# Smaller transfers and pieces at both ends, spare transposes in TensorE's waits, and other banks and operand offsets, in a kernel of two fp32 blocks

## The reference, cut to what matters

```python
def first_block(x, ...):                       # x: 256 x 2048
    h = rmsnorm(x, norm_pre_w)
    q, k, v, o_g, z_a, i_pre, f_pre, u_b, z_b, g_a, g_b = split(h @ w_in)
    q, k = silu(causal_conv4([q, k]))
    h_t = mlstm(q, k, v, i_pre, f_pre)         # 8 heads of 256
    y_a = sigmoid(o_g) * rmsnorm_head(h_t) * silu(z_a)
    y_b = (window_means(u_b) @ pool_w) * pool_scale * silu(z_b)
    merged = sigmoid(g_a) * (y_a @ w_proj_mlstm) + sigmoid(g_b) * (y_b @ w_proj_pool)
    return x + rmsnorm(merged @ w_out, norm_post_w)

def second_block(x, ...):
    h = concat(meta_tokens, x)                 # 272 tokens
    a_q, a_k, a_v, a_g, b_cq, b_ckv, b_kr, b_g = split(rmsnorm(h, attn_norm_w) @ w_in)
    oA = differential_attention(a_q, a_k, a_v) * silu(a_g)
    q = rmsnorm(b_cq, mla_q_norm_w) @ w_uq     # 512 -> 8 x (128 + 64)
    k, v = rmsnorm(b_ckv, mla_kv_norm_w) @ w_ukv   # 256 -> 8 x (128 + 128)
    oB = mla_attention(q, k, rope(b_kr), v) * silu(b_g)
    return rmsnorm(h + concat(oA, oB) @ w_out, final_norm_w)[16:]
```

## Time and profile before

| | |
|---|---|
| median of three runs (lowest, highest) | 1486.39 us (1485.68, 1487.58) |
| the profiled execution | 1488.19 us, its span 1486.3 |
| VectorE busy | 847.9 us, 57% |
| ScalarE busy | 703.4 us, 47% |
| GpSimd busy | 63.6 us, 4% |
| DMA | 265.93 MB, mean 179 GB/s |

### The profile page before, as it was taken

How to read it: one execution, slowest core, us unless ns; L and a number is a source line. 1 busy time by engine, 2 the same in 40 slices (tenths; PEclk the granted TensorE clock), 3 DMA queues, 4 the chain that set the end, 5 groups by cost and what they waited for, 6 DMA issues and landing times.

```text
span 1486.3 us, 27770 instructions
## 1 busy us (share of the span) xinstructions
PE 1452.8 (98%) x10834; PEld 1374.0 (92%) x10834; DVE 847.9 (57%) x1047; ACT 703.4 (47%) x921; POOL 63.6 (4%) x90
## 2 busy tenths in 40 slices
PE   7999999999999999999999999999999989999997
PEld 6999988899999999999999998879999978888786
DVE  5667755545665666454554545565454545656754
ACT  5544545455555534434434434455333344666542
POOL 0000000001100000000000000000000001221000
PEclk9999999999999999999999999999999999999999
DMA  7556555655555655665565557556555543333563
GB/s 279 171 198 201 177 176 168 218 176 174 175 167 193 194 178 172 188 193 186 187 194 186 188 189 274 183 190 212 165 160 169 174 150 93 102 104 114 203 208 127
DMA packets 71071, 265.93 MB, mean 179 GB/s; under 512 B 7992, under 2 KB 8000, under 8 KB 69824
## 3 DMA queue, kind: packets, MB, share of 16 engines
q1 hardware_dynamic: 69552, 254.17, 53.3%
q0 software_dynamic: 1440, 10.63, 2.0%
HBM read 260.56 MB, written 4.20 MB: 178 GB/s over the span
## 4 chain that ended last, share of the span: by engine, by line
PE 95%; DVE 2%; ACT 1%; issue 1%; DMA 0%; DVEq 0%; POOL 0%; ACTq 0%; SPq 0%; POOLq 0%
PE ps L351 23%; PE ps L353 23%; PE ps L355 23%; PE ps L341 6%; PE ps L343 6%; PE ps L342 6%; PE ps L457 2%; PE ps L729 1%; PE ps L526 1%; PE ps L537 1%; PE ps L736 1%; PE ps L734 1%; DMA xn<-in_x 0%; PE ps L574 0%; PE ps L752 0%
## 5 line engine op out<-in xcount | busy, mean ns | idle before, releaser
L1186 DVE TENSOR_TENSOR wl<-raw,wh 128x1024 fp32r<-128x1024 f32 x474 | 579.3, 1226 | 514.3 <-ACT wh L878 505.2
L878 ACT ACTIVATE wh<-raw 128x1024 fp32r<-128x1024 f32 x474 | 500.2, 1061 | 564.7 <-PE ps L355 435.7
L351 PE MATMUL ps<-xh,wh 128*128 128x256 f32 x1792 | 498.4, 278 | 0.5 <-DVE xl L1203 0.5
L353 PE MATMUL ps<-xl,wh 128*128 128x256 f32 x1792 | 496.9, 277 | 0.0
L355 PE MATMUL ps<-xh,wl 128*128 128x256 f32 x1792 | 496.8, 277 | 0.0
L351 PEld LDWEIGHTS ps<-xh,wh 128*128 128x128 f32 x1792 | 336.8, 188 | 0.8 <-DVE xl L1203 0.8
L353 PEld LDWEIGHTS ps<-xl,wh 128*128 128x128 f32 x1792 | 336.9, 188 | 0.1
L355 PEld LDWEIGHTS ps<-xh,wl 128*128 128x128 f32 x1792 | 336.8, 188 | 0.0
L351 PE MATMUL ps<-x2h,wh 128*128 128x256 f32 (+1 forms) x688 | 198.6, 289 | 4.0 <-DVE ak L1337 1.8
L353 PE MATMUL ps<-x2l,wh 128*128 128x256 f32 (+1 forms) x688 | 195.1, 284 | 0.0
L355 PE MATMUL ps<-x2h,wl 128*128 128x256 f32 (+1 forms) x688 | 194.9, 283 | 0.0
(11 more groups left out here) (324 smaller groups left out, 1769.0 us busy)
## 6 DMA issues: line engine op xcount, KB each, us to landing
raw<-in_w_stream SPq DMA_DIRECT2D x474, 512.0 KB, 3.9
xn<-in_x SPq DMA_DIRECT2D x2, 1024.0 KB, 6.2
xr<-in_x POOLq DMA_DIRECT2D x1, 2048.0 KB, 12.3
x_kept<-xr POOLq DMA_DIRECT2D x1, 2048.0 KB, 8.3
x1r<-x_kept POOLq DMA_DIRECT2D x1, 2048.0 KB, 9.8
out<-yn SPq DMA_DIRECT2D x4, 512.0 KB, 2.7
mrow<-bound_rows POOLq DMA_DIRECT2D x8, 128.0 KB, 3.3
poolw<-in_pool_w POOLq DMA_DIRECT2D x1, 1024.0 KB, 6.4
```

The costliest lines, as they stand in the source:

```text
L351: pe.matmul(out_at(j), whr[:, c, f], hi(kc)[:, tokens], start=st, stop=False, skip_group_check=True)
L353: pe.matmul(out_at(j), whr[:, c, f], lo(kc)[:, tokens], start=False, stop=False, skip_group_check=True)
L878: act.activation(slot_view(wh_at[r], layout), raw[r][:, :, :], ACT.Copy).then_inc(wh_done, 1)
L1186: tt(slot_view(wl_at[r], layout), raw[r][:, :, :], slot_view(wh_at[r], layout).bitcast(F32), ALU.subtract).then_inc(split_done, 1)
```

## The change

- Operand offsets: `LAYOUT_OF` alone sets a slot's start and pitch. `pa` and `pb` take x's layout, `ckv`, `ak`, `av` and `aq` one layout for all their slots. `yh`, `yl`, `zh`, `zl` get x's ramp; `zh` starts 192 bytes lower (`R_Z`), and with it `ol`, `gates` and others there; `four` writes four tiles of such a tensor, the first four at their own pitch, so OZ's second pass is written out rather than looped.
- Start: x comes in four transfers of 128 x 1024, `small` behind the first. ScalarE squares 1024 columns at a time, VectorE scales pieces of 512. TensorE turns 12 spare tiles of `ident` once `small` is there (`warm`), then blocks 0 to 2 of the first half, 4 spare ones, block 0 of the second half; blocks 1 and 2 of it move behind slot 0, block 3 of both behind slot 1. VectorE splits slot 0 and makes low parts ahead of the last two pieces.
- Middle: 14 spare transposes after the first half's two blocks, 14 after the second half's.
- AK, AV: the last slot of a group runs by columns, a semaphore tells that columns 0 and 1 are summed, and VectorE copies them then.
- UQ, UKV: other banks, and semaphores of their own (`s_uk_kept`, `s_uv_kept`, `s_rotation_used`).
- End: VectorE multiplies three quarters of the columns by the final weight during W2. At the end ScalarE scales the first 1024 columns in pieces of 512 and stores them from its own queue, VectorE does the other two pieces and SyncE stores them.
- Some semaphores that nothing waits for are gone, two are joined.

```diff
+LAYOUT_OF = {"qk": ON_RAMP, "o": ON_RAMP, "z": ON_RAMP, "u": ON_RAMP, "zb": ON_RAMP, "ga": ON_RAMP, "gb": ON_RAMP, "pa": ON_RAMP, "pb": ON_RAMP,
+             "v": TOKEN_RAMP, "wo": BY_TOKEN, "uv": BY_TOKEN, "w2": BY_TOKEN, "cq": SECOND_KEYS, "ckv": SECOND_KEYS,
+             "ak": SECOND_KEYS, "av": SECOND_KEYS, "aq": SECOND, "g": SECOND}
-    if kind == "pa":
-        return (0, 512) if k < 2 else (8 * k - 16, 516)
-    if kind in ("ckv", "ak", "av"):
-        return ((0, 524), (24, 524), (48, 528), (16, 528))[k if k < 2 else 2 + k % 2]
-    if kind == "aq":
-        return ((16, 524), (40, 524), (0, 528), (32, 528))[k if k < 2 else 2 + k % 2]
...
+UK_BANKS, UV_BANK = ((0, 1, 2, 3), (6, 7, 0, 1)), (2, 5)
-    R_X, R_C, R_Y, R_Z, R_V, R_T = 51200, 86016, 118784, 152064, 168448, 184896
+    R_X, R_C, R_Y, R_Z, R_V, R_T = 51200, 86016, 118784, 151872, 168576, 185024
+    def four(t, i):
+        first, pitch = (0, S + RAMP[1]) if isinstance(i, int) and i == 0 else (i * 4 * S + RAMP[4], S)
+        return t[:, bass.ds(first, 4 * pitch)].rearrange("p (c n) -> p c n", n=pitch)[:, :, 0:S]
-    yh = sb("yh", [P, KC, S + 4], F32R, R_Y)
+    yh = sb("yh", [P, KC * S + RAMP[KC]], F32R, R_Y)
-    zh = sb("zh", [P, KC // 2, S], F32R, R_Z)
+    zh = sb("zh", [P, KC // 2 * S + RAMP[KC]], F32R, R_Z)
...
+            js = range(1 if tiles else cols // P)
+            by_columns = half and k == kcs // SLOT_KC - 1
+            for c, j in [(c, j) for j in js for c in range(SLOT_KC)] if by_columns else [
+                    (c, j) for c in range(SLOT_KC) for j in js]:
...
+                    if by_columns and (c, j) == (SLOT_KC - 1, 1):
+                        last.then_inc(half, 1)
...
+        for c in range(4):
+            m, q = c // 2, slice(c % 2 * 1024, c % 2 * 1024 + 1024)
+            sp.dma_start(xn[:, m, q], x[m * P:(m + 1) * P, q]).then_inc(s_x[c], 16)
+            if c == 0:
+                sp.dma_start(small[:, :], small_in).then_inc(s_small, 16)
...
-        last_block = [(m, 3) for m in range(TOK)]
-        by_feature(xn, s_x_normed, s_x_turned, [(m, b) for m in range(TOK) for b in range(3)])
+        def warm(n):
+            for _ in range(n):
+                turn(ps[:, 0, 0:P], ident)
+
+        pe.wait_ge(s_small, 16)
+        warm(12)
+        by_feature(xn, s_x_normed, s_x_turned, [(0, 0), (0, 1), (0, 2)], 4)
+        warm(4)
+        by_feature(xn, s_x_normed, s_x_turned, [(1, 0)], 4)
...
             if j == 0 and k == 1:
-                pe.wait_ge(s_x_low, 2)
-                by_feature(xn, s_x_normed, s_x_turned, last_block)
+                by_feature(xn, s_x_normed, s_x_turned, [(1, 1), (1, 2)], 4)
+            if j == 0 and k == 2:
+                by_feature(xn, s_x_normed, s_x_turned, [(0, 3), (1, 3)], 4)
...
-        by_feature(xr, s_x1, s_x2_turned, [(0, 0), (0, 1), (1, 0)], 4)
+        by_feature(xr, s_x1, s_x2_turned, [(0, 0), (0, 1)], 4)
+        warm(14)
+        by_feature(xr, s_x1, s_x2_turned, [(1, 0)], 4)
+        warm(14)
...
-            pe_group(pe, n, [(psum_free[j % 2], uses[j % 2], 0)], half_bank(j % 2), (plain(cqh), plain(cql)), None, slice(0, S),
-                     kcs=4, ring=n % RING)
+            pe_group(pe, n, [(psum_free[j], uses[j], 0)] if j < 2 else [(s_avn, 2, 0)], half_bank(j),
+                     (plain(cqh), plain(cql)), None, slice(0, S), kcs=4, ring=n % RING)
...
-            pe_group(pe, n, both(), whole_bank(0, L2), (plain(ckh), plain(ckl)), None, slice(0, L2), kcs=2, ring=n % RING)
+            pe_group(pe, n, [(s_uk_kept, 1, 2)] if j else both(), lambda f: ps[:, UK_BANKS[j][f], 0:L2],
+                     (plain(ckh), plain(ckl)), None, slice(0, L2), kcs=2, ring=n % RING)
...
+            pe_group(pe, n, [(s_uk_kept, 3, 1)] if j else [(s_uk_kept, 2, 0), (s_rotation_used, 1, 2)],
+                     whole_bank(UV_BANK[j]), (plain(ckh), plain(ckl)),
+                     [slice(t * P, (t + 1) * P) for t in range(3)], None, kcs=2, ring=n % RING)
...
-        pe.wait_ge(psum_free[0], uses[0])
-        pe.wait_ge(psum_free[1], uses[1])
+        pe.wait_ge(s_uk_kept, 4)
+        pe.wait_ge(s_uv_kept, 1)
         gate_group(0)
...
         for m in range(TOK):
-            act.wait_ge(s_x[m], 16)
-            act.activation(xsq[:, m, :], xn[:, m, :], ACT.Square, accum_out=stat[:, m:m + 1]).then_inc(s_x_squares, 1)
+            for h in range(2):
+                q = slice(h * 1024, h * 1024 + 1024)
+                act.wait_ge(s_x[2 * m + h], 16)
+                act.activation(xsq[:, m, q], xn[:, m, q], ACT.Square, scale=D ** -0.5,
+                               accum_out=stat[:, 4 + 2 * m + h:5 + 2 * m + h])
+            act.drain().then_inc(s_x_squares, 1)
...
         for m in range(TOK):
             y_squares(3, m)
+            act.wait_ge(s_y_rstd, m + 1)
+            act.wait_ge(s_y_weighted, 3)
+            for c in range(2):
+                q = slice(c * COLS, (c + 1) * COLS)
+                act.activation(yn[:, m, q], yn[:, m, q], ACT.Copy, scale=stat[:, 22 + m:23 + m]).then_inc(s_y_scaled_too, 1)
+                act.wait_ge(s_y_scaled_too, 2 * m + c + 1)
+                act.dma_start(out[m * P:(m + 1) * P, q], yn[:, m, q]).then_inc(s_out, 16)
...
+        x_rstd(0)
+        x_scale(0, range(4))
+        x_rstd(1)
+        x_scale(1, range(2))
+        split(0, 0, LAYOUTS[0])
+        x_low_parts(0)
+        x_scale(1, range(2, 4))
+        split(1, 1, LAYOUTS[1])
+        x_low_parts(1)
+        split(2, 2, LAYOUTS[2])
+        x_low_parts(2)
+        x_low_parts(3)
...
             if kind in ("ak", "av") and k == 0:
-                dve.wait_ge(slots_done, done)
+                dve.wait_ge(s_keys_half, (2 if kind == "av" else 0) + j + 1)
                 to = ak if kind == "ak" else avt
                 for b in range(2):
+                    if b == 1:
+                        dve.wait_ge(slots_done, done)
...
+            if kind == "w2" and k == 3:
+                q = i * 2 + j
+                dve.wait_ge(s_y_squares, 2 * q + 2)
+                dve.wait_ge(s_final_w_in, 16)
+                c = slice(q * COLS, (q + 1) * COLS)
+                tt(yn[:, :, c], yn[:, :, c], finalw[:, c].unsqueeze(1).to_broadcast([P, TOK, COLS]),
+                   ALU.mult).then_inc(s_y_weighted, 1)
...
-            for q in (slice(0, D // 2), slice(D // 2, D)):
-                stt(out=yn[:, m, q], in0=yn[:, m, q], scalar=stat[:, 22 + m:23 + m], in1=finalw[:, q],
-                    op0=ALU.mult, op1=ALU.mult).then_inc(s_y_scaled, 1)
+            c = slice(2 * COLS, 3 * COLS)
+            ts(yn[:, m, c], yn[:, m, c], stat[:, 22 + m:23 + m], None, ALU.mult).then_inc(s_y_scaled, 1)
+            c = slice(3 * COLS, D)
+            stt(out=yn[:, m, c], in0=yn[:, m, c], scalar=stat[:, 22 + m:23 + m], in1=finalw[:, c],
+                op0=ALU.mult, op1=ALU.mult).then_inc(s_y_scaled, 1)
```

142 lines of the change are left out of this document (68 added, 74 removed).

## The result

The changed kernel takes 1477.79 us (median of four runs, 1476.01 to 1479.36) beside 1486.04 for the kernel before (four runs, 1485.36 to 1487.58): a ratio of 0.9943, 95% interval 0.9925 to 0.9960. It is faster, as forecast, but by 8.3 us and not by 15.9, and the time lies outside the range of 1466 to 1476.

What follows compares the result with a forecast made beforehand. TensorE's matmuls cover 98% of the span, so its waits, clock and pace bound the kernel. Terms -4.0 - 7.4 - 2.9 + 2.0 - 2.7 - 0.9 = -15.9 take the median from 1486.39 to 1470.5 us, range 1466 to 1476.

Steps and rivals of the forecast that it cites:

- (a) of the start: Start: x's second half is all there at 9.2 as before and could be turned some 1.2 us sooner.
- Step (b): Start: TensorE, turning pieces at the slow clock until 12.6, begins its first large matmul at about 15.5 instead of 15.84.
- Step (c): Start: later turns delay the chain of splits, slot 3 has its weights at 27.3; the whole start +2.0 us.
- The middle: Into CKQ: 14 spare transposes in each of two waits keep the clock at full rate; -2.9 us.
- Rival 1: Spare transposes do not hold the clock: nothing gained in the middle, first slots start slow; 1474.4 us, chance 0.12.
- Keys: AK and AV: VectorE's earlier copy of columns 0 and 1 shortens four waits of TensorE; -4.0 us.
- small projections: UK, UV and the step into G: four waits for ScalarE's copies go, 5.8, and the clock stays up, 1.6; -7.4 us.
- Placement: Operand offsets: y and pa get the scheme of x and ga, -2.7; pb -0.3, W2's ol +0.3; sum -2.7 us.
- Rival 2: Operand placement gives nothing because the pace hangs on something else; 1473.2 us, chance 0.14.
- The end: After the last rms: the first store leaves 0.9 sooner, the megabyte streams for the same 2.9 us; -0.9 us.
- Rival 3: The start does not lose, splits hidden or x sooner: -0.5 instead of +2.0; 1468.0 us, chance 0.13.
- Rival 4: Slower than before: TensorE idles at the start, QK runs on at 1.2 GHz for over 32 us; chance 0.02.

Runs made afterwards that it cites:

- s_hold: The changed kernel with 14 more spare transposes between block 0 of x's second half and the first matmul: 1476.25 us.
- m_cold: The changed kernel without the 28 spare transposes in the middle: 1479.20 us.
- best1: The changed kernel with x in two transfers, blocks 1 and 2 turned before the first matmul, pooled tensors at their old place, ScalarE's single end store: 1470.08 us.
- g_wait: The changed kernel, but ahead of G TensorE waits for the copy of both uv groups instead of the first alone: 1479.77 us.
- p_z: The changed kernel with the pooled branch's zh, zl, the bases R_Z, R_V, R_T and pb's weight layout as before: 1477.15 us.
- p_one: The changed kernel with x's tile 0 at 48 bytes behind a multiple of 128 and all others at 64: 1484.86 us.
- e_store: The changed kernel, but at the end ScalarE scales its 1024 columns in one instruction and stores them with one transfer: 1478.35 us.
- p_flat: The changed kernel with a constant ramp of 64 bytes from the first tile on for x, y and z: 1496.14 us.

## Why the prediction was right or wrong

**The step that failed is (a) of the start**: "The second half of x is all there at 9.2 as before (the bytes are the same)". The bytes are, the rate isn't: 291 GB/s instead of 407 in the first microseconds. ScalarE's last square starts at 11.71 us in the changed kernel, where the step wanted 9.2. Step (b), the first matmul at 15.5, falls with it (17.80); with two transfers it was 15.21. Step (c), the chain of splits behind the later turns, was right in kind and predicted the wait at slot 3, which is there (1.2). Its 24.7 for TensorE's own arrival there is a slip: 15.5, the 9.5 of before and eight more turns (0.87) make 25.9. Missing in (b) and (c) was a term: a low clock in slot 0, behind an idle stretch of TensorE, 1.35 us by s_hold. The two account for the start: slot 3 was to have its weights at 27.3, 11.8 behind the first matmul; it had them at 31.10, 13.3 behind, so the first matmul is 2.3 late and slot 0's clock costs 1.5, 3.8 in all, the whole way from the +2.0 forecast to the +5.8 measured. The clock was named in the bounds ("first slots also at 1.2 GHz", +4), yet even that bound lies 1.8 below the 5.8 measured, because every bound rested on x at 9.2.

**The middle** came as forecast, -2.8 for -2.9, but m_cold gives the spare transposes 1.5 of it. Rival 1 falls: they raise and hold the clock. In s_hold the clock was full from 17.2 on, ahead of any large matmul (17.96), in best1 from 10.6 (first large matmul 15.84), where transposes go from 0.213 to 0.11 us apart. By the Trainium skill's "TensorE: Matmul & The Clock Gate", section "Part 4: PE-mode transpose", it should not have engaged; the traces decide.

**Keys** (-4.3 for -4.0) and **small projections** (-7.7 for -7.4) came as worked out, waits and all. The 1.6 for the clock was put down to the last wait; in g_wait this wait alone didn't do it.

**Placement.** Pa's -2.7 came as 4 times 0.66, -2.6, by reading two groups of equal work. W2's +0.3 was mis-sized, +1.0 measured, just above its bound of 0.9, and G's +0.6 was not costed at all: the text moved zh's base and followed only ol. The -0.3 for pb gave 0.1. Rival 2 falls: p_z and p_one move the pace of equal work by placement alone. The Trainium skill's "SBUF — State Buffer", section "Who interferes with whom", says that TensorE never waits on anyone; no run here shows it waiting for another engine's access, but it doesn't follow, as the prediction took it, that placement is free.

**The end**, -0.2 for -0.9. The first store did leave earlier, 3.51 us behind the last matmul instead of 4.30. The step "the megabyte then streams for the same 2.9 us" was wrong: from the first store's issue to the last landing it took 4.52 us instead of 3.91, the last store being issued 1.89 us behind the root and its rows 2 KB long. e_store, which mends both for ScalarE's half, gets 4.09.

**From the sum to the median.** The sum was made against the profiled execution and carried over whole. That execution had the low clock in the middle and at G; at the median, 2.2 us lower, part of it is not there to be saved, as far as the clocks of the other executions tell.

Rival 3 (the start loses nothing) is the opposite of what happened. Rival 4 named the idle stretch and its low clock; the stretch lasted 3.4 us and not the 32 that the rival needed.

## What to carry to other kernels

Splitting a transfer isn't free even at equal bytes and full engines: read GB/s beside the DMA share for the new form before its landing time enters a sum, and look at when the last engine's part lands. Where several parts of a start are late together, undo each alone and both together; here 2.6 and 4.4 were worth 5.9. A base that moves by 192 bytes moves every tensor placed from it: list all matmul operands there, not the one in mind. And before a low clock in one profile is priced, look at the granted clock of the other executions: it may be in some of them only.

## What was not expected of the hardware

- Two paces of a matmul of 256 columns with equal offsets, 0.1133 and 0.1178 us, that carry over from group to group (p_flat, p_one). The ramp that looks like a detail of layout is what brings TensorE back to the fast one, in all groups but QK's first, at 0.25 us a group; without it (p_flat) the last matmul came 14.3 us later.
- Between 3 and 8 us x of 128 x 2048 comes at 427 GB/s, as 128 x 1024 pieces at 291, both halves at once at 363, as 64 x 2048 pieces at 243, with DMA shares of 0.90 to 1.03 throughout. The 291 end at about 8 us (391 behind), but by then single DMA engines are up to 2.4 us behind the others, and each transfer waits for them.
- The kernel before's executions differ by 2.9 us with the mean granted clock, 0.995 or 0.998.
- Transposes alone raise the granted clock to 1.00 (best1 at 10.6 us, s_hold at 17.2).
